# Chunked recurrence: the values' and the state's share of a step become one product over 128 partitions

## The reference, cut to what matters

```python
def step(S, inp):
    r_t, w_t, kk_t, b_t, k_t, v_t = inp
    S = (S * w_t[..., None, :]
         - jnp.einsum('dbhvk,dbhk->dbhv', S, kk_t)[..., None] * b_t[..., None, :]
         + v_t[..., None] * k_t[..., None, :])
    return S, jnp.einsum('dbhvk,dbhk->dbhv', S, r_t)
S, y = lax.scan(step, state0, xs)      # d: forwards, and over the reversed tokens
```

## Time and profile before

| | |
|---|---|
| median of 3 runs | 2534.96 us (2534.52 to 2537.42) |
| profiled execution: its time, its span | 2525.96 us, 2524.2 us |
| TensorE: matmul busy, load busy | 2158.9 us (86%), 1823.0 us (72%) |
| VectorE, ScalarE, GpSimd busy | 1291.5 us (51%), 905.5 us (36%), 723.2 us (29%) |
| mean granted clock of TensorE | 0.923 of full speed |
| stage of the recurrence | about 676 to 1202 us of the span |

### The profile page before, as it was taken

One profiled execution on the slowest core, in us unless ns is written; L12 is line 12 of the kernel. 1 busy time (PEld: TensorE's weight loads), 2 busy tenths in 40 slices (PEclk: granted clock), 3 DMA queues, 4 the chain that ended last, 5 costly groups with the idle time before them and its releaser, 6 DMA issues. The chain is left out here.

```text
span 2524.2 us, 57280 instructions
## 1 busy us (share of the span) xinstructions
PE 2158.9 (86%) x24254; PEld 1823.0 (72%) x24254; DVE 1291.5 (51%) x2064; ACT 905.5 (36%) x1765; POOL 723.2 (29%) x786
## 2 busy tenths in 40 slices
PE   3899997798179999998699994993899969999988
PEld 1666885576169989998588884773787758888866
DVE  4335467976435555554354444975546424444322
ACT  2223144455245555553133332223333303333311
POOL 2246322211143342431050001443457415000012
PEclk6999998899589999999699996996999979999989
DMA  8555444553422122110421106534344453111062
GB/s 300 184 145 155 132 146 147 187 175 120 149 77 79 54 79 78 55 58 16 96 92 34 43 13 195 182 115 162 109 114 103 112 140 117 51 51 51 32 205 92
DMA packets 207036, 280.46 MB, mean 111 GB/s; under 512 B 39640, under 2 KB 145016, under 8 KB 205760
## 3 DMA queue, kind: packets, MB, share of 16 engines
q1 hardware_dynamic: 168736, 171.52, 22.4%
q0 software_dynamic: 25680, 81.58, 10.2%
q10 hardware_dynamic: 12368, 23.70, 3.1%
HBM read 188.78 MB, written 87.95 MB: 110 GB/s over the span
## 5 line engine op out<-in xcount | busy, mean ns | idle before, releaser
L164 PE MATMUL in_acc<-in_hi,in_whi 128*128 128x512 f32 (+1 forms) x1024 | 401.3, 392 | 19.9 <-DVE in_lo L840 17.9
L164 PE MATMUL in_acc<-in_lo,in_whi 128*128 128x512 f32 (+1 forms) x1024 | 380.3, 371 | 0.0
L164 PE MATMUL in_acc<-in_hi,in_wlo 128*128 128x512 f32 (+1 forms) x1024 | 380.1, 371 | 0.0
L164 PEld LDWEIGHTS in_acc<-in_hi,in_whi 128*128 128x128 f32 x1024 | 199.5, 195 | 72.7 <-issue 42.5
L164 PEld LDWEIGHTS in_acc<-in_lo,in_whi 128*128 128x128 f32 x1024 | 199.7, 195 | 35.4 <-issue 5.3
L164 PEld LDWEIGHTS in_acc<-in_hi,in_wlo 128*128 128x128 f32 x1024 | 198.9, 194 | 33.3
L1935 DVE TENSOR_REDUCE dense_top<-dense_score 128x1 f32<-128x640 f32 (+1 forms) x144 | 112.3, 780 | 163.1 <-PE dense_score L2022 163.1
L1935 DVE TENSOR_REDUCE window_top<-window_score 128x1 f32<-128x640 f32 (+1 forms) x128 | 101.2, 791 | 179.5 <-PE window_score L2018 179.5
L2060 PEld LDWEIGHTS dense_outs<-dense_V,dense_p 128*128 128x128 f32 x1344 | 170.3, 192 | 8.5 <-ACT dense_p L1903 4.9
L2060 PE MATMUL dense_outs<-dense_V,dense_p 128*128 128x65 f32 x1344 | 170.7, 270 | 0.9 <-ACT dense_p L1903 0.8
L2060 PE MATMUL window_outs<-window_V,window_p 128*128 128x65 f32 x1216 | 157.6, 273 | 1.6 <-ACT window_p L1903 1.1
(11 more groups left out here) (269 smaller groups left out, 5085.6 us busy)
## 6 DMA issues: line engine op xcount, KB each, us to landing
streams<-in_streams_out POOLq DMA_DIRECT2D x40, 512.0 KB, 3.8
scan_L<-streams SPq DMA_DIRECT2D x80, 256.0 KB, 3.7
in_wl<-in_w_mod ACTq DMA_DIRECT2D x32, 512.0 KB, 4.4
in_raw<-in_w_in_even SPq DMA_DIRECT2D x28, 512.0 KB, 4.3
in_raw<-in_w_in_odd SPq DMA_DIRECT2D x20, 512.0 KB, 3.8
close_ga<-gates SPq DMA_DIRECT2D x18, 512.0 KB, 4.3
in_wm<-in_w_mod SPq DMA_DIRECT2D x8, 1024.0 KB, 12.2
gates<-in_outs POOLq DMA_DIRECT2D x32, 256.0 KB, 3.5
```

Of the source, the lines that this page charges most:

```text
L164: last = pe.matmul(out, a(k), b(k), start=(k == 0 and x == 0), stop=(k == n - 1 and x == 2))
```

## The change

The state is no tile of its own any more: for each direction and chunk, the values lie on one partition half of `V` and the state before that chunk on the other half, in the same columns. In the same way `EQ` is gone, and `U` holds, for each chunk, the weights of the values on one half and those of the state on the other. A step then has two kinds of product instead of three: P's as before with 64 rows, and one with 128 rows for values and state together. To place these halves, some tiles swap partition halves (`RI`, `wend`, the destination of `eq_one`, the halves of `sums` that are read as output and as state), `eq` becomes two VectorE instructions of 64 x 512 each, `V` is loaded in two pieces a direction, and the zeroing of the state becomes four loads. The diff, cut to its core:

```diff
-        state = st.sb("state", [P, 2, 2, 4, HD])
-        V = [st.sb(f"V{s}", [P, 2, 2 * P]) for s in range(6)]
+        V = [st.sb(f"V{s}", [P, 2, 2, 2 * P]) for s in range(6)]
...
-        EQ = [st.sb(f"EQ{s}", [P, NU, P]) for s in range(2)]
-        U = [st.sb(f"U{s}", [P, NU, 2, P]) for s in range(4)]
+        U = [st.sb(f"U{s}", [P, NU, 4, P]) for s in range(4)]
...
         def unit(h, d, g):
+        def place(c, b):
+            return 2 * b + c
+
...
                 def load_values(j):
-                        sp.dma_start(V[s][:, d], vtok[tile(j, d) * P:(tile(j, d) + 1) * P, 2 * r * P:2 * (r + 1) * P]
-                                     ).then_inc(v_in[s], 16)
+                        for c in range(2):
+                            row = tile(j, d) * P + c * CHUNK
+                            sp.dma_start(V[s][half_of(c), d, c], vtok[row:row + CHUNK, 2 * r * P:2 * (r + 1) * P]).then_inc(v_in[s], 16)
...
-                                sp.dma_start(RI[s][half_of(c), u:u + 2, half_of(1 - c)],
+                                sp.dma_start(RI[s][half_of(1 - c), u:u + 2, half_of(c)],
-                sp.dma_start(state[:].rearrange("p a b c n -> p (a b c n)"), consts[:, C_ZERO:C_ZERO + 16 * HD]).then_inc(zero_in, 16)
+                for r in range(2):
+                    for d in range(2):
+                        sp.dma_start(V[r][half_of(1 - d), d, d], consts[0:HD, C_ZERO:C_ZERO + 4 * HD]).then_inc(zero_in, 16)
-                                        sp.dma_start(wend[half_of(1 - c), d, r, h, g, :],
+                                        sp.dma_start(wend[half_of(c), d, r, h, g, :],
...
-                            to = U[j % 4][half_of(c), :, f - 1, half_of(1 - c)]
+                            to = U[j % 4][half_of(c), :, place(c, f - 1), half_of(c)]
...
-                            last = act.activation(RI[j % 3][half_of(c), 4 * h:4 * h + 4, half_of(c)].rearrange("p (d g) n -> p d g n", g=2),
+                            last = act.activation(RI[j % 3][half_of(1 - c), 4 * h:4 * h + 4, half_of(1 - c)].rearrange("p (d g) n -> p d g n", g=2),
...
-                                              sums[d][half_of(c), x].rearrange("p (h g) v -> p h g v", h=2), ACT.Copy)
+                                              sums[d][half_of(1 - c), x].rearrange("p (h g) v -> p h g v", h=2), ACT.Copy)
...
-                    reads = U[j % 4][:].rearrange("p (h q) b n -> p h (q b) n", h=2)
-                        dve.tensor_tensor(reads[half_of(c), :, 4 * d:4 * d + 4, half_of(c)], seen[half_of(c), :, :, 0],
+                        reads = U[j % 4][:].rearrange("p (h q) (b e) n -> p h (q b) e n", h=2, e=2)[:, :, :, c]
+                        dve.tensor_tensor(reads[half_of(c), :, 4 * d:4 * d + 4, half_of(1 - c)], seen[half_of(c), :, :, 0],
...
-                    dve.tensor_tensor(EQ[s][:, us], (small, wide)[x][s][:].rearrange("p (u a) n -> p u (a n)", a=2),
-                                      RI[j % 3][:, us], ALU.add).then_inc(eq_read, 1)
+                    eqs = (small, wide)[x][s][:].rearrange("p (u a) n -> p u (a n)", a=2)
+                    for c in range(2):
+                        half = half_of(1 - c)
+                        last = dve.tensor_tensor(U[j % 4][half, us, place(c, 1), :], eqs[half], RI[j % 3][half, us], ALU.add)
+                    last.then_inc(eq_read, 1)
...
-                        half = half_of(1 - (x ^ d))
-                        decays = wend[half, d, r, :, :, tile(j, d)].rearrange("p h g -> p (h g)")
-                        last = dve.tensor_tensor(state[half, d, r], sums[d][half, x],
-                                                 decays[:, :, None].to_broadcast([HD, 4, HD]), ALU.mult)
+                        c = x ^ d
+                        half = half_of(c)
+                        state = V[(j + 2 * x) % 6][half, d, 1 - c].rearrange("p (g h n) -> p h g n", g=2, h=2)
+                        last = dve.tensor_tensor(state, sums[d][half, x].rearrange("p (h g) n -> p h g n", h=2),
+                                                 wend[half, d, r, :, :, tile(j, d)][:, :, :, None].to_broadcast([HD, 2, 2, HD]), ALU.mult)
...
             def _(pe):
-                def values_of(j, u, half):
+                def values_of(j, u, c, rows):
-                    return V[j % 6][half, d, (g * 2 + h) * HD:(g * 2 + h + 1) * HD]
+                    return V[j % 6][rows, d, c, (g * 2 + h) * HD:(g * 2 + h + 1) * HD]
...
                 def eq_one(j, x, u, c):
-                    return pe.matmul(dst[half_of(c), u, :], PD[s][half_of(c), 4 * x + u, 0:HD],
-                                     U[j % 4][half_of(c), 4 * x + u, 0, :], start=True, stop=True)
+                    return pe.matmul(dst[half_of(1 - c), u, :], PD[s][half_of(c), 4 * x + u, 0:HD],
+                                     U[j % 4][half_of(c), 4 * x + u, place(c, 0), :], start=True, stop=True)
...
                 def av_one(j, u, c):
-                                     values_of(j, u, half_of(c)), start=True, stop=True)
+                                     values_of(j, u, c, half_of(c)), start=True, stop=True)
                 def eq_and_av(j, other):
-                        pe.wait_ge(v_in[other % 6], (other // 6 + 1) * 32)
+                        pe.wait_ge(v_in[other % 6], (other // 6 + 1) * 64)
...
                 def z(j, x):
-                    s, r = j % 2, j % 2
+                    s = j % 2
-                            pe.wait_ge(zero_in, 16)
+                            pe.wait_ge(zero_in, 64)
-                            for n in range(3):
-                                for d in range(2):
-                                    u, half = unit(h, d, g), half_of(x ^ d)
-                                    to = sums[d][:, x, h * 2 + g, :]
-                                    if n == 0:
-                                        pe.matmul(to, U[j % 4][half, u, 0, :], PD[s][half, u, HD:P], start=True, stop=False)
-                                    elif n == 1:
-                                        pe.matmul(to, U[j % 4][half, u, 1, :], values_of(j, u, half), start=False, stop=False)
-                                    else:
-                                        last = pe.matmul(to, EQ[s][half, u, :], state[half, d, r, h * 2 + g, :], start=False, stop=True)
+                            for d in range(2):
+                                u, c = unit(h, d, g), x ^ d
+                                pe.matmul(sums[d][:, x, h * 2 + g, :], U[j % 4][half_of(c), u, place(c, 0), :], PD[s][half_of(c), u, HD:P],
+                                          start=True, stop=False)
+                            for d in range(2):
+                                u, c = unit(h, d, g), x ^ d
+                                last = pe.matmul(sums[d][:, x, h * 2 + g, :], U[j % 4][:, u, place(c, 1), :],
+                                                 values_of(j, u, c, slice(0, P)), start=False, stop=True)
```

## The result

The changed kernel takes 2605.36 us (median of 4, 2603.72 to 2610.47) against 2534.74 us before on the same chip (four runs here): ratio 1.0285, interval 1.0268 to 1.0302, so 71 us slower. I had said 2580 in a range of 2558 to 2595: the right side, and 25 us too little. The profiled execution took 2603.72 us, its span is 2601.9 us, 77.7 more than before's. That is more than 71 because the profiled execution of before lies 8.8 us under its median and that of after 1.6 us under its own.

A forecast was written before the change was run, and what follows sets the result against it. TensorE's written order was taken to bound the recurrence stage. Terms 40.5 + 0 + 0.7 + 3.4 + 1.0 = +45.6 us on the profiled 2525.96, with the median's 9.0 us carried over, gave 2580 us, range 2558 to 2595.

The forecast's parts named there:

- Fewer products: In each step, 16 passes of 128 rows replace 8 blocks, 1.79 us against 1.78: 0.00 us a step.
- Changes of form: Seven switches between 64-row and 128-row passes inside each step, 0.145 us each: 1.01 us a step, +40.5 us over 40 steps.
- SP's queue: At the start, added loads of `V` and zeroing delay group 2's streams, for which TensorE waits: +3.4 us.
- VectorE's `eq`: Two half-size instructions cost 1.37 us more a group, hidden behind VectorE's waits; only at the end a step waits: +0.7 us.
- The rest: Moves between partition halves on ScalarE, GpSimd and in VectorE's `read` keep sizes and counts: 0 us.
- The clock: Rival: emptier steps lower the granted clock in a quarter of the steps, adding 33 us, 2613 us in all; chance 0.05.
- The end of the stage: In the last step, at the lower clock from about 1198 us, the added 1.01 us costs about double: +1.0 us.
- Is it hidden?: Whether TensorE's idle time from 750 to 1150 us absorbs the longer steps: 0 absorbed, 12.8 us as the bound.
- my own bound of 0.21 a change: Upper bound for one switch of row form inside a step, 0.21 us instead of 0.145: +59 us in all.

The follow-up runs named there:

- run 3: Changed kernel with the order of the two product kinds turned round for every second (h, g), four changes of form a step instead of seven: 2577.20 us, ratio 1.0184.
- run 5: Changed kernel with P's products also taken over all 128 rows, against zeroes written once by GpSimd: 2582.28 us, ratio 1.0211.
- run 1: Kernel before with one edit, `eq_one`'s product sent to columns 1 - c as in the changed kernel: 2545.81 us, ratio 1.0057.
- run 2: Changed kernel with `eq_one` put back to columns c, seven changes of form a step kept: 2600.36 us, ratio 1.0282.
- run 6: Changed kernel with four changes of form a step instead of seven and `eq_one` put back to columns c: 2561.40 us, ratio 1.0145.
- run 4: Kernel before with each product of every step cut into two of 64 columns, 96 passes of form 64*64: 2559.41 us, ratio 1.0115.
- run 8: Kernel before with the products of only the first step of each group cut into two of 64 columns: 2537.62 us, ratio 1.0032.

## Why the prediction was right on the side and wrong on the size

*Fewer products: right.* The 128-row pass costs 0.11 us, as much as the two that it replaces and that ran side by side, so it gains nothing; in longer stretches of one form it costs the same (runs 3 and 5).

*Changes of form: right.* Seven at 0.145 us were forecast, 1.01 a step; the trace has 1.00, run 3 removes three of them and 0.42 us. That is 40 us. The Trainium skill ("TensorEngine Tiling (Array Packing)", Key Properties) says that changing the tiling mode drains TensorE. The trace agrees and shows the price that the page leaves open: the next weights come 0.20 us after the last pass's start.

*SP's queue: right in kind, and in size partly by luck.* 3.4 forecast, 2.8 measured at the wait, 3.4 at the first step. The added loads alone took 4.8, and quicker decay loads gave some of it back. *VectorE's `eq`:* hidden, and 0.7 at the end, both as forecast.

*The step that failed* is "The rest. Moves between partition halves keep sizes and counts", priced at 0. I counted instructions of ScalarE, GpSimd and VectorE, and never asked which quadrant of the array (which half of its rows with which half of its columns) TensorE's own 64\*64 products use. `eq_one` read rows c and wrote columns c; `y_one` and `av_one`, between which it is interleaved, go from rows c to columns 1 - c. The change moves `eq_one` to columns 1 - c, so two quadrants stand empty and the two kinds queue in the other two. In the trace this costs 0.86 us a period, in the 18 periods behind the first step in which a `y_one` stands beside it, so 15.5 us. Alone, in the kernel before, it cost 14 us (10 to 19, run 1). The stretch with `av_one` grows as well, from 1.04 us (768.27 to 769.31, before) to 1.80 (868.74 to 870.54, run 1). It costs nothing: TensorE waits behind it for GpSimd's masks, and from second step to next first step both kernels take 12.36 or 12.37 us.

*The clock.* I gave it 0.05, as a rival at 33 us. It happened in a smaller size: nine falls of 3.4 us, 1.5 us each where two periods can be compared, so 13 us. The two kernels with seven changes a step (after and run 2) have falls; those with four or none (runs 3, 5 and 6) have none between 750 and 1150 us. So, among these kernels, the falls come with the seven changes. (Run 4, without changes but with TensorE standing still up to 3.1 us at a time, has falls too.) TensorE's busy time doesn't tell them apart: 399.7 of 400 us in the kernel after, 399.6 in run 5. How seven changes bring them about, and why run 2 has more of them, stays open; each run also has another period, and no run changes the period alone. My argument against the rival, that the rest of the period is dense, failed: in run 2 the rest of TensorE's period is as in the kernel before, and the clock falls some 16 times.

*The end of the stage.* I gave the lower clock there +1.0 us, for the last step alone. It holds for both last steps of the kernel after and costs 5.4 us, against 1.0 before: +4.4.

*Is it hidden?* I took 0 absorbed, with 12.8 as the bound. The first 16 periods show 4.6 us of idle time in the kernel before that are gone after.

The sum for the profiled executions is 40 for the steps, 15.5 for `eq_one`, 13 for the falls, 3.4 at the start, 0.7 for the last `eq` and 4.4 at the end, less 4.6 absorbed: 72.4 of the 73 us up to the last pass. The two terms that I had at nothing, `eq_one` and the falls, are some 28 of the 32 us between my 45.6 and the 77.7. The range shares the fault: it put neither of them in, and its upper end of 2595 lies under what my own bound of 0.21 a change gives (59 instead of 40.5, so 2599).

## What to carry to other kernels

Before merging small matrix products, look at the starts of the passes: where two already start together on opposite halves of the array, a product over all rows only takes the place of both, and each change between row forms costs time of its own, 0.14 us here. When an operand moves to the other partitions, write down rows and columns of each product beside it in the order; quadrants are a resource as much as time is. And give the lower clock a term of the sum of its own: here it cost 13 us inside the stage and 4.4 at its end.

## What the runs showed of the hardware that I had not expected

- The number of changes of form decides, and not only what the passes are: 16 unpaired passes and 16 paired ones in eight stretches take 3.62 us, all 32 unpaired in one form 3.50.
- Over 400 us TensorE got some 65 instructions a us (64.9 and 65.4 in runs 4 and 8), loads and matmuls counted together; shorter stretches reach more (888 + 888 in the 24 us from 876 us, 74 a us, in run 4). The kernel before is at 62.5, so cutting its products into more passes gained nothing; a step of the cut form did run in about 1.5 us when it wasn't interrupted (run 4, from 989.46 to 991.03).
- The granted clock fell for 3.4 us at a time in a kernel whose TensorE is busy 399.7 of 400 us by its records, and it didn't in one that is busy 399.6.
- The same crossed `eq_one` costs 14 us in one kernel and next to nothing in another: the period is 0.86 us longer in both, but in the second the kernel with it has some ten falls of the clock fewer.
